# Stage boundaries of a two-block transformer kernel: freeing the input slice by slice, high parts first, another bank order

## The reference

```python
h = rms_norm(x, norm_in_g); proj = h @ w_in          # stage "in", 32 tiles
h = x + concat(y_pool, y_mlstm) @ w_out              # "wo_pool", "wo_m", 8 tiles each
x = rms_norm(h, norm_out_g)
...
for i in range(2):
    h = rms_norm_2(x, norm_mix[i])
    if i == 0: x = x + nsa_mixer(h, ...)             # "nsa" 21 tiles in, "nsa_o" 8 tiles out
    else:      x = x + swa_mixer(h, ...)             # "swa" 10 tiles in, "swa_o" 8 tiles out
    h = rms_norm_2(x, norm_ffn[i])
    a, u = split(h @ w_gu)                           # "gu0", "gu1": 44 tiles
    x = x + (silu(conv(a)) * u) @ w_down             # "down0", "down1": 22 slices
return rms_norm_2(x, norm_final)
```

## Time and profile before

| what | value |
|---|---|
| median of 3 runs | 1775.37 us (1775.35 to 1777.21) |
| the profiled execution | 1770.42 us, of which span 1768.6 us |
| PE busy | 1653.4 us, 93% of the span |
| DVE, ACT, POOL busy | 1019.4, 604.9, 647.2 us |
| share of the span on PE in the chain that ended last | 81% |
| mean granted clock of PE | 0.975 of full speed |

### The profile page before, as it was taken

How to read it: one execution, slowest core, us unless ns; L and a number is a source line. 1 busy time by engine, 2 the same in 40 slices (tenths; PEclk the granted TensorE clock), 3 DMA queues, 4 the chain that set the end, 5 groups by cost and what they waited for, 6 DMA issues and landing times.

```text
span 1768.6 us, 21435 instructions
## 1 busy us (share of the span) xinstructions
PE 1653.4 (93%) x8324; PEld 1292.0 (73%) x8324; DVE 1019.4 (58%) x1406; ACT 604.9 (34%) x1160; POOL 647.2 (37%) x421
## 2 busy tenths in 40 slices
PE   6999998979989799999999999999799999999996
PEld 4888665657878666677888887878567788887884
DVE  6994344565895466634655554448762555555444
ACT  4222332444121366534222222234463422222223
POOL 2444211144441133234444443443234444443442
PEclk9999999989999999999999999999899999999998
DMA  6222100024220000012222222232101222222221
GB/s 228 98 92 97 70 24 24 24 75 154 95 99 34 28 2 1 2 36 84 95 96 96 100 102 73 100 114 72 49 1 60 83 96 98 103 97 84 95 96 48
DMA packets 37669, 133.84 MB, mean 76 GB/s; under 512 B 4608, under 2 KB 5056, under 8 KB 37056
## 3 DMA queue, kind: packets, MB, share of 16 engines
q1 hardware_dynamic: 34992, 123.22, 20.1%
q10 hardware_dynamic: 2576, 9.24, 1.4%
HBM read 130.35 MB, written 2.10 MB: 75 GB/s over the span
## 4 chain that ended last, share of the span: by engine, by line
PE 81%; DVE 10%; ACT 4%; issue 3%; POOL 2%; ACTq 0%; DMA 0%; DVEq 0%; POOLq 0%
PE ps L1394 17%; PE ps L1396 17%; PE ps L1395 17%; PE ps L1704 5%; PE ps L1705 4%; PE ps L1706 4%; PE ps L1639 3%; PE ps L1654 3%; PE ps L1675 2%; PE ps L1423 2%; PE ps L1667 1%; DVE sb_arena L1073 1%; POOL sb_w_lo L374 1%; PE ps L1511 1%; ACT sb_arena L639 1%
## 5 line engine op out<-in xcount | busy, mean ns | idle before, releaser
L374 POOL TENSOR_TENSOR sb_w_lo<-sb_raw,sb_w_hi 128x1024 fp32r<-128x1024 f32 x227 | 556.6, 2452 | 896.4 <-ACT sb_w_hi L408 896.4
L1394 PE MATMUL ps<-sb_x_hi,sb_w_hi 128*128 128x512 f32 x1464 | 582.0, 398 | 37.1 <-ACT sb_x_hi L426 13.3
L1396 PE MATMUL ps<-sb_x_hi,sb_w_lo 128*128 128x512 f32 x1464 | 576.4, 394 | 0.0
L1395 PE MATMUL ps<-sb_x_lo,sb_w_hi 128*128 128x512 f32 x1464 | 576.0, 393 | 0.0
L408 ACT CAST sb_w_hi<-sb_raw 128x1024 fp32r<-128x1024 f32 x227 | 238.7, 1051 | 667.8 <-PE ps L1396 483.3
L1394 PEld LDWEIGHTS ps<-sb_x_hi,sb_w_hi 128*128 128x128 f32 x1464 | 278.8, 190 | 107.2 <-issue 20.0
L1396 PEld LDWEIGHTS ps<-sb_x_hi,sb_w_lo 128*128 128x128 f32 x1464 | 278.5, 190 | 59.2
L1395 PEld LDWEIGHTS ps<-sb_x_lo,sb_w_hi 128*128 128x128 f32 x1464 | 279.0, 191 | 58.3 <-issue 1.2
L1283 DVE TENSOR_TENSOR sb_x_lo<-sb_arena,sb_x_hi 128x512 fp32r<-128x512 f32 x44 | 97.6, 2230 | 117.2 <-ACT sb_x_hi L700 117.2
L1704 PE MATMUL ps<-sb_x_hi,sb_w_hi 128*128 128x512 f32 x352 | 139.1, 395 | 8.7 <-DVE sb_x_lo L1283 8.7
L1705 PE MATMUL ps<-sb_x_lo,sb_w_hi 128*128 128x512 f32 x352 | 138.6, 394 | 0.0
(11 more groups left out here) (235 smaller groups left out, 1724.6 us busy)
## 6 DMA issues: line engine op xcount, KB each, us to landing
sb_raw<-in_w SPq DMA_DIRECT2D x227, 512.0 KB, 3.2
sb_resid<-in_x SPq DMA_DIRECT2D x8, 256.0 KB, 5.8
sb_arena<-in_cmp_w1k ACTq DMA_DIRECT2D x1, 2048.0 KB, 10.7
sb_arena<-in_cmp_w1v ACTq DMA_DIRECT2D x1, 2048.0 KB, 15.3
out<-sb_resid SPq DMA_DIRECT2D x8, 256.0 KB, 2.1
sb_arena<-in_pool_w ACTq DMA_DIRECT2D x1, 1024.0 KB, 4.8
sb_arena<-in_invc ACTq DMA_DIRECT2D x1, 1024.0 KB, 6.9
sb_arena<-in_wg ACTq DMA_DIRECT2D x1, 768.0 KB, 8.3
```

The costliest lines, as they stand in the source:

```text
L374: nc.gpsimd.tensor_tensor(WL[:, w % SPL], raw[:, w % RAW], WH[:, w % SPL].bitcast(F32), ALU.subtract).then_inc(tile_split, 1)
L1394: mm(out, WH[:, s, k], XH[:, k], start=(k == 0), stop=False)
L1395: mm(out, WH[:, s, k], XL[:, k], start=False, stop=False)
L1396: ins = mm(out, WL[:, s, k], XH[:, k], start=False, stop=(k == KT - 1))
```

## The change

Four things change, all at the places where one stage ends and the next begins.

1. In the last tile of `wo_m`, `nsa_o`, `gu0`, `swa_o` and `gu1` PE signals `x_free` after each slice, and ACT overwrites `XH[:, k]` as soon as slice `k` has been read, in place of waiting for the tile. The last slice waits for the residual add of the last tile, which DVE now does after five of the eight `XL` slices. For `down`, ACT makes the first four high parts before the last silu, and DVE the first low part before the last `gu` product is taken out.
2. The first tile of `wo_pool`, `wo_m`, `nsa`, `gu0`, `swa`, `gu1` and the first slice of `down0` and `down1` run the 16 matmuls on `XH` first and the 8 on `XL` behind them.
3. In the second tile of `nsa`, `gu0`, `swa` and `gu1` the order is `WH XH`, `WH XL`, `WL XH`. It starts on `hi_made`, and POOL makes that tile's `WL` only after all eight `XL` slices are ready.
4. The last slice of `down` goes through the banks in the order 4, 5, 6, 7, 2, 3, 0, 1 (`LEFT`), and `R` is added, multiplied, split and (at the end) squared in that order. After `down0` ACT no longer waits for the tile, and its two loads of `cos` and `sin` move from the end of `down0` to its seventh slice.

```diff
+EDGES = ["wo_m", "nsa_o", "gu0", "swa_o", "gu1"]
+LAST_TILE = {"wo_m": KT - 1, "nsa_o": KT - 1, "gu0": 2 * FT - 1, "swa_o": KT - 1, "gu1": 2 * FT - 1}
+GATED = ["nsa", "gu0", "swa", "gu1"]
+LEFT = [4, 5, 6, 7, 2, 3, 0, 1]
+def x_left(stage, k):
+    return (KT - 1) * EDGES.index(stage) + k + 1
...
             for w in range(NW):
+                for stage in GATED:
+                    if w == W0[stage] + 1:
+                        pool.wait_ge(xl_ready, X0[stage] + KT)
                 pool.wait_ge(hi_made, w + 1)
...
-            def times_gain(ready, gain, used=0):
-                if used:
-                    act.wait_ge(tile_used, used)
-                for k in range(KT):
-                    act.wait_ge(*ready(k))
+            def times_gain(ready, gain, behind=None, order=range(KT)):
+                for n, k in enumerate(order):
+                    if behind and k < KT - 1:
+                        act.wait_ge(x_free, x_left(behind, k))
+                    act.wait_ge(*ready(n))
                     nc.scalar.mul(XH[:, k], R[:, k], col(gain, k)).then_inc(xh_ready, 1)
...
                 for f in range(1, FT):
                     high(w0 + 2 * f + 2)
+                    if f == FT - 1:
+                        for n in range(4):
+                            act.wait_ge(x_free, x_left(f"gu{layer}", n))
+                            hidden_high(n)
                     silu(0 if f == 1 else f)
                     high(w0 + 2 * f + 3)
...
-                act.wait_ge(tile_used, wd)
-                for f in range(4):
-                    hidden_high(f)
...
-            act.wait_ge(tile_used, W0["down0"] + FT - 1)
-            for dst, name in ((cs, "cos"), (sn, "sin")):
-                act.dma_start(dst, a[name]).then_inc(consts_in, 16)
-            times_gain(lambda k: (down_added, k + 1), "g_mix1", W0["swa"])
+            times_gain(lambda n: (down_added, n + 1), "g_mix1", order=LEFT)
+            high(W0["swa"] + 1)
...
-            add_residual("nsa_o", behind=lambda k: k and add_square(3, k))
-            split_rest("gu0", "g_ffn0")
+            add_residual("nsa_o", tiles=range(KT - 1), behind=lambda k: k and add_square(3, k))
+            split_rest("gu0", "g_ffn0", range(5))
+            add_residual("nsa_o", tiles=[KT - 1])
+            split_rest("gu0", "g_ffn0", range(5, KT), 5)
+            add_square(3, KT - 2)
             add_square(3, KT - 1)
...
-                pe.wait_ge(tile_split, w + 1)
+                pe.wait_ge(*((hi_made, w + 1) if j == 1 and stage in GATED else (tile_split, w + 1)))
                 s = w % SPL
+                order = LEFT if stage == "swa" else range(KT)
+                if j == 0 and stage != "in" and stage not in MERGED:
+                    for n_, k in enumerate(order):
+                        pe.wait_ge(xh_ready, X0[stage] + n_ + 1)
+                        mm(psum(BANK[t]), WH[:, s, k], XH[:, k], start=(n_ == 0), stop=False)
+                        mm(psum(BANK[t]), WL[:, s, k], XH[:, k], start=False, stop=False)
+                    for n_, k in enumerate(order):
+                        pe.wait_ge(xl_ready, X0[stage] + n_ + 1)
+                        ins = mm(psum(BANK[t]), WH[:, s, k], XL[:, k], start=False, stop=(n_ == KT - 1))
...
+                    if LAST_TILE.get(stage) == j and k < KT - 1:
+                        ins.then_inc(x_free, 1)
...
```

More of the change, by code:

```diff
@@ L558, in _ @@
                 two_squares(k)
-            times_gain(lambda k: (freed, T0["wo_m"] + k + 1), "g_mix0", W0["nsa"])
+            times_gain(lambda k: (freed, T0["wo_m"] + k + 1), "g_mix0", "wo_m")
             high(W0["wo_m"] + KT + 1)
@@ L696, in ffn @@
                         silu(1)
-                def hidden_high(f):
-                    act.wait_ge(mid_ready, layer * FT + f + 1)
-                    nc.scalar.copy(XH[:, f % 4], MID[:, f]).then_inc(xh_ready, 1)
-                act.wait_ge(tile_used, wd)
-                for f in range(4):
-                    hidden_high(f)
-                for f in range(FT):
-                    high(wd + f + 2)
+                for f in range(FT):
+                    if f < FT - 1:
+                        high(wd + f + 2)
+                    if f == 6 and layer == 0:
+                        act.wait_ge(xl_ready, X0["down0"] + 4)
+                        for dst, name in ((cs, "cos"), (sn, "sin")):
+                            act.dma_start(dst, a[name]).then_inc(consts_in, 16)
                     if f + 4 < FT:
@@ L744, in _ @@
             residual_squares("swa_o", 5)
-            times_gain(lambda k: (freed, T0["swa_o"] + k + 1), "g_ffn1", W0["gu1"])
+            times_gain(lambda k: (freed, T0["swa_o"] + k + 1), "g_ffn1", "swa_o")
             ffn(1, 5)
-            for k in range(KT):
-                act.wait_ge(down_added, KT + k + 1)
-                if k == 7:
+            for n, k in enumerate(LEFT):
+                act.wait_ge(down_added, KT + n + 1)
+                if n == 7:
                     act.wait_ge(sq_acc, 7 * 6 + 1)
-                nc.scalar.activation(SQ6[k] if k < 4 else RMS if k == 4 else SQ[:, k % 2], R[:, k], ACT.Square
+                nc.scalar.activation(SQ6[n] if n < 4 else RMS if n == 4 else SQ[:, n % 2], R[:, k], ACT.Square
                                      ).then_inc(sq_ready, 1)
@@ L764, in _, with split_rest @@
             step = Steps(dve, dve_step)
-            def split_rest(x, gain):
-                for k in range(KT):
-                    dve.wait_ge(xh_ready, X0[x] + k + 1)
+            def split_rest(x, gain, order=range(KT), at=0):
+                for n, k in enumerate(order):
+                    dve.wait_ge(xh_ready, X0[x] + at + n + 1)
                     nc.vector.scalar_tensor_tensor(XL[:, k], R[:, k], col(gain, k), XH[:, k].bitcast(F32),
@@ L1039, in behind_wo_m @@
                     step.mark(nc.vector.memset(BDK, 0.0))
-            add_residual("wo_m", behind=behind_wo_m)
+            add_residual("wo_m", tiles=range(KT - 1), behind=behind_wo_m)
             dve.wait_ge(gains_ready, 1)
-            split_rest("nsa", "g_mix0")
+            split_rest("nsa", "g_mix0", range(5))
+            add_residual("wo_m", tiles=[KT - 1])
+            split_rest("nsa", "g_mix0", range(5, KT), 5)
+            add_two_squares(KT - 2)
             add_two_squares(KT - 1)
@@ L1306, in ffn @@
                     hidden(f)
-                for f in range(4):
+                for f in range(1, 4):
                     rest(f)
@@ L1311, in ffn @@
                         rest(f + 4)
[L1312 to L1314 removed]
+                for n, k in enumerate(LEFT):
+                    if n < KT - 1:
+                        dve.wait_ge(down_mm, (KT - 1) * layer + n + 1)
                     else:
@@ L1344, in _ @@
             attention(SWA_UNITS, len(NSA_UNITS), True)
-            add_residual("swa_o", "b_o", behind=lambda k: k and add_square(5, k))
-            split_rest("gu1", "g_ffn1")
+            add_residual("swa_o", "b_o", tiles=range(KT - 1), behind=lambda k: k and add_square(5, k))
+            split_rest("gu1", "g_ffn1", range(5))
+            add_residual("swa_o", "b_o", tiles=[KT - 1])
+            split_rest("gu1", "g_ffn1", range(5, KT), 5)
+            add_square(5, KT - 2)
             add_square(5, KT - 1)
```

49 lines of the change are left out of this document (36 added, 13 removed).

## The result

The changed kernel takes 1747.88 us (median of four runs, 1746.04 to 1752.6) where the kernel before takes 1775.36 (four runs, 1774.44 to 1777.21): ratio 0.9858, 95% interval 0.9839 to 0.9876, so 27.5 us or 1.4% faster. The forecast was 1751.5, range 1746 to 1760.

A forecast was written before the change was run, and what follows sets the result against it. PE, 93% busy, was taken to lose 33.9 us at six stage boundaries, standing still and then at low clock. Terms 5.0 + 3.9 + 7.1 + 0.5 + 4.1 + 5.6 - 2.3 = 23.9 us off 1775.37 gave 1751.5, range 1746 to 1760.

The forecast's parts named there:

- 3.9 and 4.1: Gains forecast at `gu0` and `gu1`: a stall of 0 to 0.6 us, with the clock staying up.
- the 0.35 us set aside at each `down` for GpSimd's split: Half of a possible 0.7 us delay from POOL's second `WL`, leaving gains of 7.1 at `down0` and 5.6 at `down1`.
- for 0.5: Gain taken for `swa`, as its third tile waits for POOL's `WL`; cases from -0.7 to 2.4.
- 3 to 4 were forecast: In `swa`, a PE wait of 3 to 4 us between second and third tile, for POOL's `WL`.
- the forecast's other case: `swa` gains 2.4 if the clock stays up, against 0.2 if the low clock comes back.
- for 2.3: Loss forecast at `wo_m`: 0.8 from eight low matmuls behind the last slice, up to 2.2 more from the low clock.
- the bound of 3.0: Worst end of the loss forecast at `wo_m`, whose bounds were 0.8 and 3.0.
- The forecast was 5.0: Gain at `nsa`: the 5.5 us lost there less 0.5 of stall, down to 4.1 if the third tile's `WL` is delayed.
- ACT is idle from 427.16: At `nsa`, seven high slices take ACT to 431.5, and slice 7 comes at 432.8 against 432.3 wanted by PE.
- 23.9: Total gain forecast in us, over `nsa`, `gu0`, `down0`, `swa`, `gu1` and `down1`, less the loss at `wo_m`.
- rival 2: POOL's gate makes PE wait in second tiles of `gu0`, `gu1`, `nsa`: gain 18.9 down to 12.3, 1756.5 to 1763.1; 10%.
- The 2.2 us of clock per boundary: At six stage boundaries, the part of the loss laid to PE's low clock after standing still, some 13 us.

The follow-up runs named there:

- e1: The changed kernel once more, with no edit, as the yardstick of its group of runs: 1748.4 us, ratio 0.9854.
- e2: The changed kernel with only the first tiles of `wo_pool` and `wo_m` back in the order of before: 1746.25 us, ratio 0.9845.
- e3: The changed kernel with ScalarE's two squares of slice 6 after `wo_m` moved behind the high slices for `nsa`: 1746.89 us, ratio 0.9846.
- e5: The changed kernel with the edits of e2 and e3 together: 1746.9 us, ratio 0.9852.
- e7: The changed kernel with every first tile, including the first of `down`, in the order of before; freeing slice by slice stays: 1743.88 us, ratio 0.9842.
- e8: The changed kernel without GpSimd's wait (the gate) before the second tile's low half at `nsa`, `gu0`, `swa`, `gu1`: 1749.29 us, ratio 0.9871.
- e6: The changed kernel without the freeing slice by slice and the ScalarE and VectorE orders that go with it; high first stays: 1756.91 us, ratio 0.9917.
- e9: The changed kernel without freeing slice by slice and with every first tile in the order of before: 1769.54 us, ratio 0.9975.
- e10: The changed kernel with second tiles of `nsa`, `gu0`, `swa`, `gu1` in the order of before and without GpSimd's gate: 1755.45 us, ratio 0.989.
- e4: The kernel before, with useless matmuls filling PE's wait before the first tile of `nsa`, `gu0`, `down0`, `gu1`, `down1`: 1767.78 us, ratio 0.9973.
- e11: e4 with the second tile of `nsa`, `gu0`, `swa`, `gu1` in the changed kernel's order: 1763.2 us, ratio 0.9937.
- e12: e7 with, in `swa`, ScalarE's third-tile cast behind its fourth square and the norm's matmul inside the third tile: 1745.94 us, ratio 0.984.

## Why the prediction was right, and where it was not

**`gu0`, `gu1`: right.** 4.0 and 4.5 for 3.9 and 4.1, no stall, full clock.

**`down0` with `swa`, `down1`: right in kind, 1.0 and 0.5 us too low.** `down0` gains 7.5, all there was: the 0.35 us set aside at each `down` for GpSimd's split did not come, and no wait stands at the second slice. `swa` has 1.1 in the changed kernel and -0.2 in e1, for 0.5. There PE waits 1.44 us for the sums and 1.39 for GpSimd between the second and third tile, 2.8 where 3 to 4 were forecast, and in the profiled run the low clock came with it, as forecast. Where it did not (e2, e3), `swa` gains 2.5, the 2.4 of the forecast's other case.

**`wo_m`: right in kind.** A loss of 2.8 and 2.3 in two profiles for 2.3, at the low clock: the eight low products take 3.41 us (1.8 at full rate). With what the low clock costs in the second tile, 0.4 us, it is 3.2 in the changed kernel, a little over the bound of 3.0.

```profile
392.92 0.80 PE L1421 MATMUL ps<-sb_x_hi,sb_w_hi 128*128 128x512 f32 x1 [0.46 <-ACT sb_x_hi L553]
393.94 3.62 PE L1425 MATMUL ps<-sb_x_lo,sb_w_hi 128*128 128x512 f32 x8
397.35 0.63 PE L1444 MATMUL ps<-sb_x_hi,sb_w_hi 128*128 128x512 f32 x1
```

**`nsa`: the step that failed.** The forecast was 5.0, the profile has 2.3 (2.7 without `wo_m`'s tail). The step was "ACT is idle from 427.16". It took ScalarE's last squares from the profile of before, where VectorE's sum got in ahead of GpSimd's split. Then that race cost nothing either way, as ScalarE waited for the old tile. The early freeing put it on the path, and in the changed kernel VectorE lost it. Where the squares are out of the way (e3, e5), or VectorE wins (e7, e8), `nsa` gains 4.6 to 4.9.

**The sum.** The stretches of the profile give 22.7 for 23.9. The median fell by 27.5. Medians of four runs scatter by some 2 us. Two things are large enough for the rest, and no run tells them apart, since only one execution of each group was profiled. If the race and `swa`'s clock fall well in most unprofiled runs, 2.3 and some 1.5 to 2.7 us are won that the profile does not have. And the 3.8 to 5.1 us that most profiles lose before the 344th us, where nothing was changed, may fall on the runs of before more often than on those of the changed kernel. So the account here holds for the 22.7; that the median came within 3.6 us of the forecast is in part luck.

**What was missing.** The sum was right, its reasons were not complete. I gave all of the gain to the early freeing. e6, e7 and e9 show that freeing and high first stand in for each other: either alone keeps PE's waits at 1.8 us or less and the clock up at `gu0`, `down0`, `gu1` and `down1`. With the rest of the change kept, the freeing alone gives all that both give; high first alone gives 16.3 of 22.7 us, neither 5.5, and high first costs 2.3 to 2.8 at `wo_m`. The gate does nothing that could be measured (e8). And the second tile, which I had only as a risk (rival 2), is a condition: without its new order 7 us of the gain are lost (e10), and a full clock by itself is waited away before it (e4, e11). The 2.2 us of clock per boundary were time that only two of five boundaries gave back when the clock alone was mended.

**Signals, and who holds off whom.** The seven added signals in a last tile cost nothing that the trace shows: `gu0`'s boundary, where they stand, gains the full 4.0, and starts in that tile stay 0.23 us apart. The Trainium skill (TensorE: Matmul & The Clock Gate, "The cost: per-tile semaphore tail") gives 26.3 ns an increment where packed tiles finish together; as an estimate, seven would cost 0.2 us. Between VectorE and GpSimd, the rows of e8 and of the changed kernel show that one of the two is held for nearly the whole of the other's instruction: 2.92 us for VectorE where it takes 0.68 alone and GpSimd's instruction 2.39, and 2.97 for GpSimd the other way round. The Trainium skill (SBUF — State Buffer, "Who interferes with whom") says that issue order decides who blocks; the rows agree that one blocks, but the order of the starts in the records, GpSimd first by 0.02 us in both, does not tell which.

## What to carry to other kernels

When a wait at a stage's edge is taken away, read the profile on through the second, third and fourth tile: the next supplier (here GpSimd's low half) is no earlier than it was, and decides how much is kept. When two edits fill the same wait, run each alone: here the change without its new first tiles is at least as fast as all of it, and simpler. An order that puts two thirds of the work first helps where inputs come at the consumer's pace, and hurts where they come slower, because the last third then stands behind the last input.

## What the hardware showed that I had not expected

- The low clock does not always follow the same wait. In `swa` PE's starts lie 1.8 us apart before the norm's two matmuls and 2.0 us behind them, in the changed kernel, in e1 and in e2, to 0.02 us; the granted clock of the 5 us behind them is 0.69 and 1.00, and 0.50 in e1, which is the changed kernel again. The rows of e1 and e2, and two waits of e9, at `gu0`, where starts 0.43 us apart follow, and at `gu1`, where they stay at 0.23:

```profile
1196.64:1201.64 5.00, 5.00 (x12) 0.50 0.54 156
1194.27:1199.27 5.00, 5.00 (x22) 1.00 0.49 155
821.67 0.47 PE L1421 MATMUL ps<-sb_x_hi,sb_w_hi 128*128 128x512 f32 x1 [2.14 <-DVE sb_x_lo L787]
1380.74 0.47 PE L1421 MATMUL ps<-sb_x_hi,sb_w_hi 128*128 128x512 f32 x1 [2.20 <-DVE sb_x_lo L787]
```
- A tie between VectorE and GpSimd, with starts 0.02 us apart, can go either way, and costs 2.3 us when the loser is on the path. It went against VectorE in the changed kernel, e1 and e2, and for it before the change and in e3, e5, e6, e7, e8, e10 and e12. Whether one and the same program can have both outcomes is not shown: the one program with two profiles, the changed kernel, lost it twice.
- A wait of 1.8 us of PE (e6, at `down0`) left its clock at 1.00, and one of 1.51 (e10, `gu0`) too; one of 2.17 (e10, `nsa`) was followed by 3.4 us of starts 0.43 apart, and so was one of 2.31 (e4, `nsa`).
